# Sample-group depthwise convolution on VectorE: 31 multiply-adds per channel tile instead of product tables and reductions

## The reference, cut to what matters

```python
u = za * jax.nn.sigmoid(zb)
conv_in = jnp.concatenate([conv_past, u], axis=1)          # 30 past steps, then the new ones
d = lax.conv_general_dilated(conv_in, conv_w[:, None, :], window_strides=(1,), padding='VALID',
                             dimension_numbers=('NWC', 'WIO', 'NWC'), feature_group_count=CONV_W) + conv_b
d = layer_norm(d, conv_ln_g, conv_ln_b)                    # over the 1024 channels
```

## Time and profile before

| | us |
|---|---|
| median of three runs | 3752.33 |
| lowest and highest | 3748.51, 3754.24 |
| the profiled execution, its own time | 3748.51 |
| its span in the profile | 3746.7 |
| PE busy | 3517.2 (94%) |
| PE weight loads busy | 3257.7 (87%) |
| DVE busy | 1797.4 (48%) |
| POOL busy | 1217.4 (32%) |
| ACT busy | 1065.2 (28%) |

### The profile page before, as it was taken

The page is one execution under the profiler, slowest core; times in us unless marked ns, Lnnn a source line. Parts: engine busy times, 40 slices in busy tenths (PEclk is TensorE's granted clock), DMA queues, the critical chain, the costliest instruction groups (busy, mean ns, idle before and its releaser), DMA issues. The chain is left out here.

```text
span 3746.7 us, 66701 instructions
## 1 busy us (share of the span) xinstructions
PE 3517.2 (94%) x27774; PEld 3257.7 (87%) x27774; DVE 1797.4 (48%) x2508; ACT 1065.2 (28%) x1494; POOL 1217.4 (32%) x476
## 2 busy tenths in 40 slices
PE   5699999989899899999998999998988999999999
PEld 2499988878889889898887999897888898889999
DVE  0422578946888412322114135789189791233311
ACT  1322222222353233221213222222233523332221
POOL 0133333543323222333232333235333232224433
PEclk9799999999999999999998999999999999999999
DMA  9733334555544675558994555442332246744442
GB/s 302 232 110 103 95 103 110 158 146 175 153 125 123 198 238 193 173 194 262 307 294 132 159 158 166 135 120 77 94 98 85 72 131 221 241 136 134 131 127 93
DMA packets 556513, 590.47 MB, mean 158 GB/s; under 512 B 73432, under 2 KB 523245, under 8 KB 546475
## 3 DMA queue, kind: packets, MB, share of 16 engines
q1 hardware_dynamic: 556212, 586.21, 51.5%
HBM read 546.37 MB, written 116.39 MB: 177 GB/s over the span
## 5 line engine op out<-in xcount | busy, mean ns | idle before, releaser
L781 POOL TENSOR_TENSOR w_lo_t<-raw,w_hi_t 128x1024 fp32r<-128x1024 f32 x472 | 1217.2, 2579 | 2512.9 <-ACT w_hi_t L790 2512.9
L1067 PE MATMUL acc<-act_hi,w_hi_t 128*128 128x272 f32 x6528 | 1414.3, 298 | 112.9 <-POOL w_lo_t L781 38.0
L1067 PE MATMUL acc<-act_hi,w_lo_t 128*128 128x272 f32 x6528 | 1361.4, 290 | 0.0
L1067 PE MATMUL acc<-act_lo,w_hi_t 128*128 128x272 f32 x6528 | 1359.9, 290 | 0.0
L1067 PEld LDWEIGHTS acc<-act_hi,w_hi_t 128*128 128x128 f32 x6528 | 1040.9, 191 | 201.2 <-issue 131.6
L1067 PEld LDWEIGHTS acc<-act_lo,w_hi_t 128*128 128x128 f32 x6528 | 1039.4, 191 | 0.0
L1067 PEld LDWEIGHTS acc<-act_hi,w_lo_t 128*128 128x128 f32 x6528 | 1032.6, 191 | 0.0
L790 ACT ACTIVATE w_hi_t<-raw 128x1024 fp32r<-128x1024 f32 x472 | 499.9, 1059 | 1665.6 <-PE acc L1067 1662.7
L1067 PE MATMUL acc<-m_hi,w_hi_t 128*128 128x272 f32 x1024 | 215.8, 292 | 0.0
L1590 DVE SCALAR_TENSOR_TENSOR conv<-conv,cw 128x512 f32<-128x512 f32 x240 | 212.2, 884 | 0.0
L1067 PE MATMUL acc<-m_hi,w_lo_t 128*128 128x272 f32 x1024 | 211.5, 288 | 0.0
(11 more groups left out here) (240 smaller groups left out, 2711.5 us busy)
## 6 DMA issues: line engine op xcount, KB each, us to landing
raw<-in_w_in_dram SPq DMA_DIRECT2D x272, 512.0 KB, 3.7
ada_ring<-in_w_ada_dram SPq DMA_DIRECT2D x94, 512.0 KB, 6.3
raw<-in_w_in_dram SPq DMA_DIRECT2D x136, 256.0 KB, 3.3
k_near<-in_cache_k_dram SPq DMA_DIRECT2D x256, 128.0 KB, 2.7
v_near<-in_cache_v_dram SPq DMA_DIRECT2D x256, 128.0 KB, 2.7
k_ring<-k_near SPq DMA_DIRECT2D x64, 512.0 KB, 5.3
v_page<-v_near SPq DMA_DIRECT2D x64, 512.0 KB, 6.1
raw<-in_w_out_dram SPq DMA_DIRECT2D x64, 512.0 KB, 4.6
```

What stands on the lines that cost most here:

```text
L781: pool.tensor_tensor(w_lo_t[:, m % 2], raw[:, m % 4], w_hi_t[:, m % 2].bitcast(F32), ALU.subtract).then_inc(S.w_lo, 1)
L1067: last = pe.matmul(acc[:, 2 * m + h, 0:HALF], w[:, c % 2, k, P * m:P * m + P], r[:, kt, h * HALF:(h + 1) * HALF], start=first and k == 0 a ...
```

## The change

In `make_u` the product tables and sums go. The sample convolution is now written as the prompt's is: for each of the 31 taps one instruction multiplies the 8 x 4 inputs of that tap by the channel's weight and adds them to the outputs. Even taps add into `d_s[:, c]` (the first also adds the bias), odd ones into a new buffer `d_s_odd`, and one addition joins them. So 4 instructions of 128 x 248 and 2 reductions of 128 x 496 per channel tile become 2 TENSOR_SCALAR, 29 SCALAR_TENSOR_TENSOR and 1 TENSOR_TENSOR of 128 x 32. The semaphore `conv_s_done` and its waits, one of them on PE, go with it, and L1747 becomes a plain copy.

```diff
+        d_s_odd = at(C + 16288, "d_s_odd", [P, NS])
...
-                if b == 0 and f == 0:
-                    pe.wait_ge(S.conv_s_done, 8 * l + 8)
...
-                products = aux[:, 2, 0:2 * SEQS * TAPS].rearrange("p (b t k) -> p b t k", b=SEQS, k=TAPS)
-                need(dve, S.conv_s_done, 8 * l + c)
-                for t0 in range(0, STEPS, 2):
-                    st.wait()
-                    for t in range(2):
-                        st.then(dve.tensor_tensor(products[:, :, t, :], us[:, s, :, t0 + t:t0 + t + TAPS],
-                                                  cw[:, l, c, :].unsqueeze(1).to_broadcast([P, SEQS, TAPS]), ALU.mult))
-                    st.wait()
-                    ins = dve.tensor_reduce(samp(d_s[:, c, :])[:, :, t0:t0 + 2], products, AX_X, ALU.add)
-                    st.then(ins) if t0 == 0 else ins.then_inc(S.conv_s_done, 1)
+                for k in range(TAPS):
+                    out = samp(d_s[:, c, :] if k % 2 == 0 else d_s_odd[:, :])
+                    src, w = us[:, s, :, k:k + STEPS], cw[:, l, c, k:k + 1]
+                    if k == 0:
+                        st.then(dve.tensor_scalar(out, src, w, par[:, l, R_CB + c:R_CB + c + 1], ALU.mult, ALU.add))
+                    elif k == 1:
+                        st.then(dve.tensor_scalar(out, src, w, None, ALU.mult))
+                    else:
+                        st.wait(back=1)
+                        st.then(dve.scalar_tensor_tensor(out=out, in0=src, scalar=w, in1=out, op0=ALU.mult, op1=ALU.add))
+                st.wait()
+                st.then(dve.tensor_tensor(d_s[:, c, :], d_s[:, c, :], d_s_odd[:, :], ALU.add))
...
-                    dve.wait_ge(S.conv_s_done, 8 * l + 8)
-                    st.then(dve.tensor_tensor(conv[:, 0:CT_, SEQ:TOK], d_s[:, :, :], bc(par[:, l, R_CB:R_CB + CT_], NS), ALU.add))
+                    st.then(dve.tensor_copy(conv[:, 0:CT_, SEQ:TOK], d_s[:, :, :]))
```

More of the change, by code:

```diff
@@ L451, in trunk_kernel @@
             state_in0 state_in1 state_used state_taken u_done u_turned u_copied u_stored0 u_stored1 state_copied
-            conv_s_done mean_in mean_ps mean_done cent_done csq_done cvar_in var_ps cstd_done ln_done silu_done gc_done yc_stored yc_back
+            mean_in mean_ps mean_done cent_done csq_done cvar_in var_ps cstd_done ln_done silu_done gc_done yc_stored yc_back
             gate_stored0 gate_stored1 gate_stored2 gate_stored3 ga_used
```

## The result

The changed kernel takes 3788.72 us, median of five runs (3786.54 to 3799.71), against 3753.16 (3748.51 to 3763.89) before. The ratio is 1.0111, with a 95% interval of 1.0094 to 1.013: 35 to 49 us slower, 42 in the middle. The forecast was 3785, 35 us of added time. The profiled execution of the changed kernel is one of the slower ones, 3799.16 us with a span of 3797.4, so it stands 50.6 above the profiled one of before.

A forecast was written before the change was run, and what follows sets the result against it. PE works nearly throughout; the changed DVE work lies where PE and DVE wait in turn and POOL stalls DVE. 10.6 + 7.1 - 0.1 = 17.6 us a layer, 35 in all, gave 3785 us, range 3762 to 3818.

The forecast's parts named there:

- The price of the small multiply-add: New sample chain on DVE: 0.25 us per 128x32 multiply-add, starts 0.17 us apart, 5.5 us a chain instead of 2.87.
- rival B: Sample chains: small multiply-adds do not overlap and take 0.29 us each, 52 us more in all, 3836 us; chance 0.11.
- The stall that comes along: Chains at tiles 0 to 3: a POOL op starts inside and stalls a two-SBUF-input DVE instruction, 2.3 us more.
- Waits for relu: PE's dot products at tiles 0 to 3 wait for ACT's relu, 2.3 to 3.0 us each, 10.6 us a layer.
- Waits for `u_s`: PE waits 2.95, 1.95 and 2.25 us more at tiles 5, 6 and 7, 7.1 us a layer.
- The clock: New PE waits of 2 to 3 us cost no clock; at worst some 4 us a layer.
- POOL's long ops: POOL ops held off by runs of 31 prompt taps, PE waiting 18.9 us a layer for `w_lo_t`: expected to stay.
- Rival C: Prompt taps: POOL's long ops go because DVE is later, giving back up to 56 us, 3729 us, faster; chance 0.07.
- L1747: Sums' transfer into `conv`, 2.50 us with a stall: becoming a copy gains between 0 and 2.5, taken as 0.1 a layer.
- Rival A: POOL's op slips behind the chain harmlessly or DVE's idle time is real room: 3 us a layer, 3755; chance 0.12.
- D: New chains hold POOL off, delaying `w_lo_t`, or clock falls: 25 us a layer, up to 3835, middle 3810; chance 0.08.

The follow-up runs named there:

- the gaps: Kernel before, with every fourth prompt tap of tiles 3 to 7 waiting for the tap just before it: 3701.58 us, ratio 0.981.

## Why the prediction was right

The sum was 17.6 us a layer. Its steps, one by one:

- *The price of the small multiply-add.* Forecast 0.25 us each and 0.17 apart, 5.5 for the chain; measured 0.244, 0.163 and 5.3. The interpolation from 128 and 512 columns and the overlap of taps carried over. The no-overlap rival B fell with it: each starts 0.08 us before the one ahead ends. The prediction set beside B the letter of the Trainium skill's page "VectorE: DVE Perf Modes", section "The DRAIN you can't avoid", that the next op does not start until the pipe is empty. The same section adds that an op that is not held starts earlier, which agrees with this trace, so the page did not speak for B. Its advice in "Rules for kernel authors" to minimize the op count stood in its direction: 32 instructions took 5.3 us where 6 took 2.87.
- *The stall that comes along.* Forecast 2.3 us at each of tiles 0 to 3, inside the chain; measured there once in each chain (2.45 at tile 1), and twice at tile 0, where the old form was stalled once and took 5.1 us, not the 2.87 that the prediction put for every tile. The runs with the sums in PSUM and with 17 taps show it from both sides. The prediction's condition, two inputs in SBUF, is too narrow: copies with one are stalled too (L1557, L1746). The Trainium skill's page "SBUF — State Buffer" (section "SBUF: two separate sides") gives the lock to a VectorE operation with two SBUF inputs or in a 2-port perf mode. The 464 instructions that were not stalled agree with its first half; in which mode the copies ran, no run here shows.
- *Waits for relu.* Forecast 2.3, 2.55, 2.75 and 3.0; measured 1.71, 2.25, 2.43 and 2.64: 9.0 us a layer for 10.6.
- *Waits for `u_s`.* Forecast 7.1 us more a layer at tiles 5, 6 and 7; measured 5.6 in layer 0 (3.58 at tile 5, 2.06 at tile 7) and 2.3 in layer 1 (tile 6). This is the weakest step: I added the stalls of an interval as if each came for certain and none could fall into what idle time was left. In layer 1 no POOL op met tile 4's chain, and DVE still stood idle 1.4 us before tile 5's states:

```profile
2523.24 0.41 DVE L1573 COPY us<-aux 128x240 f32<-128x240 f32 x1 [1.40 <-PE aux L1150]
```

- *The clock.* Forecast nothing, with 4 us a layer at worst; measured 11.9 and 6.8 in the profiled execution. This term was mis-sized, and it covered for the ones above. I had reasoned from single waits of up to 2.4 us that cost no clock in this trace. In layer 0 a second wait of about the same length now follows the first by 9 us, and the clock halves behind it (0.91 over that stretch of 20 us); in layer 1 the same pair of waits (1.72 and 2.25 us) left it at 1.00:

```profile
517.49 0.52 PE L1067 MATMUL acc<-act_hi,w_hi_t 128*128 128x272 f32 x2 [1.72 <-DVE u_s L1550]
...
526.85 0.80 PE L1139 MATMUL aux<-ki_new,qi 64*128 64x256 f32 x4 [2.25 <-ACT relu_p L886]
```

- *POOL's long ops.* Forecast to stay, three a layer: they did, 1.2 and 3.1 us longer in PE's waits. Rival C did not come by itself, and the gaps show what it is worth: 1.4 to 1.9%.
- *L1747.* Forecast 0.1 us; 2.50 became 2.37, the stall in both. Without POOL's op, in the kernel of before and the changed one with gaps, the addition takes 0.43 us and the copy 0.29, so 0.1 was right.

Rival A fell (the room was not there), D too: POOL was not held off by the small instructions, as PE's waits for it in the kernel with the chain at tiles 0 to 3 show (37.7 us, 38.0 before), and no POOL op of the changed kernel but the three of each layer lasted over 3.3 us. In all, right by its mechanism and its place. That the time came within 4 us is in part luck: in the profiled execution the waits for relu and `u_s` were some 9 us less than forecast, and 18.7 us of clock and 4.4 of `w_lo_t` had been left out. That execution lies 15 us above its forecast of 3783.7, the median 4 above 3785.

## What to carry to other kernels

Price an instruction on an engine that others follow closely by what it lasts there and by which stalls it can attract, not by the engine's mean load: DVE was idle for half of the time, and 39 us of added work (16 x 2.43) came back as 42 us; the two figures are near each other by chance, since by the run with the sums in PSUM the length alone costs about 8 us and the stall that it draws in the rest. Idle time that lies beside an operation of the other engine, as DVE's beside POOL's here, is not all room: filling it can bring the stall back. And look at a long run of instructions that overlap on one engine from the side of the engine that it can hold off: a wait on itself, a tenth of a microsecond every few instructions, was worth 1.4 to 1.9% of the whole kernel.

## What was not expected of the hardware

POOL loses to DVE not by chance but for a whole run: in runs of overlapping multiply-adds with two SBUF inputs it was kept out for 10 to 16 us (ops of 12.5 to 18.1 us, of which 2.4 are its own work) three times per layer and in some executions once more. At 716.84 us before it asked amid the taps and ran only when the joining addition L1593, which waits for the instruction before it, had come up. Elsewhere, at the same distance of 0.66 us between starts, it won at once (POOL's op at 676.34, beside the L1590 that took 2.88 us from 676.50). What tells the two apart is open; that a gap at every fourth or eighth tap ends it is shown (the longest POOL op of any kernel with gaps is 5.6 us). With it the spread of the times of the kernel before also shrinks, from 3762 to 3778 us in that set to 3700 to 3705.

Short waits can cost clock, but their sum does not say how much. With four waits for `u_s` a layer at 1.4 to 2.4 us the clock stayed at 1.00 beside them before, and with the waits for relu added it was 0.83 to 0.91 in the four stretches of layer 0 shown. In layer 1 the same waits cost it twice at tiles 0 to 3, not four times (6.8 us more lost over the layer, against 11.9). And in the kernel of before with gaps, which has the old four waits and none for relu, it fell twice in layer 1 right behind a wait for `u_s`:

```profile
2334.42 0.78 PE L1067 MATMUL acc<-act_hi,w_hi_t 128*128 128x272 f32 x2 [1.69 <-DVE u_s L1552]
```

```profile
2334.50:2337.90 3.40, 3.40 (x15) 3.40 (x16) 3.25 (x8) 0.00 (x0) 0.00 (x0) 0.50 0.69 189
```

So more waits made it likelier here, and no experiment tells what decides in the single case.
